# First mixer's output product: halves of the contraction by source, and the memory's transposes between the second halves

## The reference

```
x = x + hybrid_mixer(rms_norm(x, norm_mix_g), ...)      # [o_attention | h_mlstm] @ w_out
x = x + cross_attention(rms_norm(x, norm_x_g), rms_norm(mem, norm_mem_g), w_xq, w_xk, w_xv, w_xo)
```

## Time and profile before

| | us |
|---|---|
| median of 3 timed runs (1586.34 to 1586.98) | 1586.88 |
| the profiled execution's own time | 1581.93 |
| its span, first to last instruction | 1580.1 |
| TensorE busy in the span (matmuls) | 1350.8 |
| DVE / ACT / POOL busy | 536.6 / 413.6 / 423.5 |
| mean granted clock of TensorE, of full | 0.930 |

### The profile page before, as it was taken

One profiled execution on the slowest core, in us unless ns is written; L12 is line 12 of the kernel. 1 busy time (PEld: TensorE's weight loads), 2 busy tenths in 40 slices (PEclk: granted clock), 3 DMA queues, 4 the chain that ended last, 5 costly groups with the idle time before them and its releaser, 6 DMA issues. The chain is left out here.

```text
span 1580.1 us, 16473 instructions
## 1 busy us (share of the span) xinstructions
PE 1350.8 (85%) x6188; PEld 892.8 (57%) x6188; DVE 536.6 (34%) x1076; ACT 413.6 (26%) x796; POOL 423.5 (27%) x391
## 2 busy tenths in 40 slices
PE   6999976989889759987878888870999999999798
PEld 5777755788647633332223232220788887787466
DVE  3659657121061331111111111117141314563552
ACT  5323544144320200000000000014322223444441
POOL 7553340257410111211111111117144550000220
PEclk9999988999989759999999999995999999999799
DMA  7311212134202738999999999983132332232000
GB/s 198 107 54 55 106 54 80 59 128 148 92 4 98 315 159 337 422 420 424 420 423 421 424 421 423 422 344 120 54 107 80 107 100 81 87 105 82 1 21 34
DMA packets 72223, 297.73 MB, mean 188 GB/s; under 512 B 10152, under 2 KB 10200, under 8 KB 51424
## 3 DMA queue, kind: packets, MB, share of 16 engines
q1 hardware_dynamic: 64704, 282.27, 45.6%
q0 software_dynamic: 7456, 14.59, 2.9%
HBM read 292.63 MB, written 12.58 MB: 193 GB/s over the span
## 5 line engine op out<-in xcount | busy, mean ns | idle before, releaser
L703 POOL TENSOR_TENSOR ring_rounded<-ring,ring_rounded 128x512 fp32r<-128x512 f32 x208 | 284.9, 1404 | 326.1 <-ACT ring_rounded L1314 326.1
L826 PE MATMUL bank<-HT_rounded,ring_rounded 128*128 128x512 f32 x544 | 215.9, 397 | 4.3 <-DVE ring_rounded L1673 2.8
L1063 PE MATMUL bank<-ring,B 128*64 128x512 f32 x704 | 179.5, 663 | 44.2 <-DMA ring<-in_w 43.1
L828 PE MATMUL bank<-HT_rounded,ring_rounded 128*128 128x512 f32 x544 | 212.4, 390 | 0.0
L827 PE MATMUL bank<-ring_rounded 128*128 128x512 f32 x544 | 212.3, 390 | 0.0
L1063 PEld LDWEIGHTS bank<-ring,B 128*64 128x64 f32 x704 | 54.9, 150 | 152.4 <-issue 113.7
L828 PE MATMUL bank<-ring_rounded 128*128 128x512 f32 x352 | 137.9, 392 | 0.0
L1314 ACT ACTIVATE ring_rounded<-ring 128x2048 fp32r<-128x2048 f32 x56 | 106.4, 1915 | 111.4 <-DMA ring<-in_w_in_a 45.5
L2034 DVE TENSOR_TENSOR B<-bank,small 128x512 f32<-128x512 f32 x32 | 22.1, 692 | 331.7 <-PE bank L1053 331.7
L826 PEld LDWEIGHTS bank<-HT_rounded,ring_rounded 128*128 128x128 f32 x544 | 102.6, 189 | 32.2 <-issue 6.2
L827 PEld LDWEIGHTS bank<-ring_rounded 128*128 128x128 f32 x544 | 102.7, 189 | 21.7 <-issue 1.0
(11 more groups left out here) (362 smaller groups left out, 2034.4 us busy)
## 6 DMA issues: line engine op xcount, KB each, us to landing
ring<-in_w SPq DMA_DIRECT2D x88, 1024.0 KB, 30.3
A<-in_w SPq DMA_DIRECT2D x11, 2048.0 KB, 28.8
ring<-in_w SPq DMA_DIRECT2D x11, 2048.0 KB, 28.7
A<-in_w SPq DMA_DIRECT2D x20, 1024.0 KB, 28.8
HT<-in_w SPq DMA_DIRECT2D x20, 1024.0 KB, 32.2
XN<-in_w SPq DMA_DIRECT2D x10, 2048.0 KB, 28.9
ring<-in_w_in_a SPq DMA_DIRECT2D x16, 1024.0 KB, 5.0
ring<-in_w_in SPq DMA_DIRECT2D x14, 1024.0 KB, 7.3
```

What stands on the lines that cost most here:

```text
L703: last = pool.tensor_tensor(r32(lo), lo, r32_read(quarter(g, True)[:, k, :]), ALU.subtract)
L826: pe.matmul(o, r32(a_hi), r32(b_hi), start=first, stop=False)
L828: return pe.matmul(o, r32(a_lo), r32(b_hi), start=False, stop=last)
L1063: last = pe.matmul(bank[2 + b][64 * j:64 * j + 64, :], xgT[b][:, k, hf, :], w, start=(n == 0), stop=(n == 7), skip_group_check=True)
```

## The change

The output product's contraction is now taken by source. TensorE transposes the attention's four tiles, runs the first half of the contraction of `wo0` (channel tiles 0 to 3) for row tiles 0 to 2, transposes the cell's four tiles, runs row tile 3, then the first half of `wo1` for all four, the second half of `wo0`, the memory's transposes, and the second half of `wo1`. All eight banks are open at once in between. On DVE the attention's low parts come ahead of the cell's normalisation, and the additions of `wo1` behind the memory's low parts. On ACT the attention's high copies come ahead of the root and the memory's sums, and the memory's high copies ahead of the sums of the new x. In the plan, `opened` and `closed` become two lists, with four "skip" entries for banks that stay open.

```diff
     plan += [(("y_t", m), "dve") for m in range(8)]
-    plan += [(("wo", n, t), "dve") for n in range(2) for t in range(NT)]
+    plan += [(("wo", 0, t), "dve") for t in range(NT)]
     plan += [(("mem_t", k), "dve") for k in range(KD // 2)]
+    plan += [(("wo", 1, t), "dve") for t in range(NT)]
...
+    closed = [what for what, _ in plan]
+    opened = list(closed)
+    early = [("wo", 0, t) for t in range(NT)]
+    for what in early:
+        opened.remove(what)
+    at = opened.index(("y_t", 4))
+    opened[at:at] = early
+    late = [("wo", 1, t) for t in range(NT)]
+    for what in late:
+        opened.remove(what)
+    at = opened.index(("mem_t", 0))
+    opened[at:at] = [("skip", t) for t in range(NT)] + late
+    return opened, closed, dict(plan)
...
         last = opened[n - 8] if n >= 8 else None
+        if last and last[0] == "skip":
+            last = opened[n - 16]
...
-            for m in range(8):
+            def turn_y(m):
...
+            def out_half(outs, n, t, h):
+
+                part = weights(chunk_no[f"wo{n}"])
+                for k in range(4 * h, 4 * h + 4):
+                    last = passes(outs[t], lambda k: (yT[:, k, P * t:P * t + P], lowT[:, k, P * t:P * t + P]), part, k,
+                                  k == 0, k == KD - 1)
+                return last
+
+            for m in range(4):
+                turn_y(m)
+            outs = [[fill(U, "wo", 0, t)[:, :] for t in range(NT)]]
+            pe.wait_ge(sem("y_low_ready"), 4)
+            wait_split(pe, chunk_no["wo0"], 0)
+            for t in range(NT):
+                if t == NT - 1:
+                    for m in range(4, 8):
+                        turn_y(m)
+                last = out_half(outs[0], 0, t, 0)
+            last.then_inc(first_half_read, 1)
+            done[0] += NT
+            outs.append([fill(U, "wo", 1, t)[:, :] for t in range(NT)])
+            wait_split(pe, chunk_no["wo1"], 0)
+            for t in range(NT):
+                last = out_half(outs[1], 1, t, 0)
+            last.then_inc(first_half_read, 1)
             pe.wait_ge(sem("y_low_ready"), 8)
-            for n in range(2):
-                to_rows(f"wo{n}", U, [("wo", n, t) for t in range(NT)], yT, lowT)
-
+            wait_split(pe, chunk_no["wo0"], 1)
+            for t in range(NT):
+                out_half(outs[0], 0, t, 1).then_inc(bank_filled, 1)
...
+            wait_split(pe, chunk_no["wo1"], 1)
+            for t in range(NT):
+                out_half(outs[1], 1, t, 1).then_inc(bank_filled, 1)
             wait_emptied(pe, U["mem_t", KD // 2 - 1])
...
+            for m in range(4):
+                o = filled(U["y_t", m])
+                act.activation(r32(yT[:, m, :]), o[:, :], ACT.Copy, scale=g_sub_s).then_inc(sem("high_ready"), 1)
             roots(6, 48, 64)
...
             roots(7, NT, NT + MT)
             high_parts("xk0")
-            for t in range(NT):
-                wait_emptied(act, U["wo", 1, t])
-                sums(x_rows, t, 8 + t)
             act.wait_ge(sem("more_loaded"), 16 * 8)
...
+            for t in range(NT):
+                wait_emptied(act, U["wo", 1, t])
+                sums(x_rows, t, 8 + t)
             roots(8, 8, 8 + NT)
```

More of the change, by code:

```diff
@@ L167, in first_plan @@
     plan += [(("table",), "dve")]
-    return plan
+    closed = [what for what, _ in plan]
[11 more added lines that the diff above has]
+    return opened, closed, dict(plan)
 def second_plan():
@@ L237, in number @@
 def number(opened, closed, by, base, act0, dve0):
-    assert sorted(map(str, opened)) == sorted(map(str, closed))
+    assert sorted(str(what) for what in opened if what[0] != "skip") == sorted(map(str, closed))
     count, emptied = {"act": act0, "dve": dve0}, {}
@@ L246, in number @@
     for n, what in enumerate(opened):
+        if what[0] == "skip":
+            continue
         last = opened[n - 8] if n >= 8 else None
+        if last and last[0] == "skip":
+            last = opened[n - 16]
         after = (by[last], emptied[last]) if last else None
@@ L262, in build @@
 def build(nc, a, out):
[L264 to L267, removed]
+    opened1, closed1, by1 = first_plan()
+    n1 = len(closed1)
+    U, act1, dve1 = number(opened1, closed1, by1, 0, 0, 0)
     V, _, _ = number(*second_plan(), n1, act1, dve1)
@@ L1417, in _ @@
                 sums(mem_rows, t, NT + t)
[L1418 to L1425, removed]
+            for m in range(4, 8):
+                wait_emptied(act, U["y_t", m])
+                act.activation(r32(yT[:, m, :]), lowT[:, m, :], ACT.Copy).then_inc(sem("high_ready"), 1)
             roots(7, NT, NT + MT)
             high_parts("xk0")
-            for t in range(NT):
-                wait_emptied(act, U["wo", 1, t])
-                sums(x_rows, t, 8 + t)
             act.wait_ge(sem("more_loaded"), 16 * 8)
@@ L1833, in _ @@
                     head_rows(h - 1)
+            for m in range(4):
+                o = filled(U["y_t", m])
+                wait_high()
+                own(dve.scalar_tensor_tensor(r32(lowT[:, m, :]), o[:, :], g_sub_s, r32_read(yT[:, m, :]), ALU.mult,
+                                             ALU.subtract))
+                dve.nop().then_inc(done, 1)
+                dve.nop().then_inc(sem("y_low_ready"), 1)
             own(dve.tensor_scalar(ss[:, 48:64], mv[:, 1:32:2], float(P), None, ALU.mult))
@@ L1843, in _ @@
                 last.then_inc(sem("y_rows_ready"), 1)
-            for m in range(8):
+            for m in range(4, 8):
                 o = filled(U["y_t", m])
[L1846 to L1855, removed]
+                dve.wait_ge(sem("sig_ready"), m - 3)
+                dve.scalar_tensor_tensor(lowT[:, m, :], o[:, :], g_ml[:, m - 4:m - 3], moT[:, m - 4, :],
+                                         ALU.mult, ALU.mult).then_inc(done, 1)
             for m in range(4, 8):
@@ L1865, in _, with add_row @@
                    .then_inc(sem("memn_ready"), 1)
[L1867 to L1872, removed]
+            def add_row(name, n, t):
+                o = filled(U[name, n, t])
+                v = x_rows[:, t, 512 * n:512 * n + 512]
+                dve.tensor_tensor(v, o[:, :], v, ALU.add).then_inc(done, 1)
             dve.wait_ge(sem("x_again"), 16 * NT)
-            add_rows(U, "wo")
+            for t in range(NT):
+                add_row("wo", 0, t)
             dve.wait_ge(sem("more_loaded"), 16 * 8)
@@ L1884, in _ @@
                 last.then_inc(done, 1)
+            for t in range(NT):
+                add_row("wo", 1, t)
             rstds(NT, [(8, 8 + NT, D)])
@@ L1918, in _ @@
                                .then_inc(done, 1)
-            add_rows(U, "xw")
+            for n in range(2):
+                for t in range(NT):
+                    add_row("xw", n, t)
             rstds(NT, [(12, 12 + NT, D)])
```

## The result

| | before, us | changed, us |
|---|---|---|
| median of 5 timed runs | 1586.88 (1580.92 to 1587.98) | 1568.4 (1563.06 to 1571.4) |
| the profiled execution's own time | 1581.93 | 1563.06 |
| its span | 1580.1 | 1561.2 |
| mean granted clock | 0.930 | 0.940 |

The ratio is 0.99, 95% interval [0.9863, 0.9936]. The change gains; forecast were 13.1 us and 1573.8, with a range of 1571.3 to 1578.2.

A forecast was written before the change was run, and what follows sets the result against it. TensorE was taken as the bound except for two waits, ahead of the output product and the keys. Keys starting 11.4 us earlier plus 1.7 of kept clock gave 13.1 off 1586.88: 1573.8 us, range 1571.3 to 1578.2.

The forecast's parts named there:

- low clock behind that wait: At the output product's first matmuls after TensorE's idle wait: the lower clock costs 2.4 us, as before; ends 0 and 4.8.
- wait ahead of the keys: Before the keys' product: TensorE waits 1.4 us instead of 4.26, for DVE's fourth addition, and starts at 319.4.
- clock kept in the keys: In the keys' 192 matmuls: the short wait keeps the clock at 1.00, winning 1.7 us.
- the stages behind: After the keys: later work is tied to TensorE's own events and should move rigidly, with nothing further won or lost.
- my two ends: At the output product's start: the attention's four low parts take 4.66 us, or 4.3, winning 10.2 or 10.5 us.
- The transfer chain: Keys' weights: load from 305.5, 5.15 landing, 1.92 ACT copy, 4.17 memory copies and low parts, ending at 316.7.
- The cover for the second keys' weights: POOL's split of these weights: first half ready at 329.5, wanted at 330.9; slack 1.4 us, the next thing late.
- (a): Keys: the clock falls after the 1.4 us wait all the same; gain 11.4, 1575.5 us; chance 0.12.
- (b): Paired 1 MB loads share the engines, the first lands 2.5 us late; gain 8.9, 1578.0 us; chance 0.07.
- (c): Product's start: ACT's copies come only behind the root, DVE's first low part stays at 268.85; gain 8.1, 1578.8; chance 0.03.
- (d): Slower: the keys' load takes 30.3 us as in the expert stage; TensorE starts 13.8 us later, 1600.7; chance 0.03.
- I take 13.1 off both: Whole kernel: 13.1 us subtracted from profiled execution and timed median alike, giving 1568.8 and 1573.8 us.

The follow-up runs named there:

- the second trace: The changed kernel executed again without edits: ratio 0.9902 [0.9869, 0.9935] to the kernel before, median 1564.78 us of 6 runs, span 1569.0.
- the other three traces with before's order: Kernel before executed again, and with extra constant matmuls in two later waits (15 and 8; 8 and 5): ratios 0.9994, 1.0036, 0.9998.
- the first pair: First profiled executions of the kernel before and of the changed kernel: spans 1580.1 and 1561.2 us.
- the fillers: Extra constant matmuls in TensorE's waits; 4, 8 and 5 ahead of output product, cross attention and third norm in the changed kernel: 0.9867, median 1561.32 us.
- the parts apart: Against the kernel before: only the product by source, memory behind it as before, 0.9953; only the memory between the second halves, 0.9985.
- part 2 alone: Against the kernel before, memory's transposes between the second halves, all eight y tiles still transposed and split ahead of the product: 0.9985, median 1577.09 us.

## Why the prediction was right and wrong

**The mechanism and its size held.** The table gives the forecast's terms against what the runs showed, shifted by the 0.68 us of upstream where it is an instant.

| step | forecast | measured |
|---|---|---|
| start of the product | 268.5, 10.2 us won (10.5 as the bound) | 268.20, 10.5 us won |
| low clock behind that wait | 2.4 us (0 to 4.8) | 1.9 to 2.3 |
| both sets of transposes in the stream | 1.8 + 1.8 | product ends at about 317.9 (forecast 318.0) |
| wait ahead of the keys | 1.4, DVE's addition to X | 1.23 (1.60 in the second trace) |
| keys' start | 319.4 | 319.08 |
| clock kept in the keys | 1.7 | 1.5 (24.62 to 23.10); 1.3 against the other three traces with before's order |
| the stage | 13.1 | 13.2 in the first pair, 12.5 in the mean |
| the stages behind | 0, they "move rigidly" | 5.0 won in the first pair, 8.3 lost in the second |

That the first pair gives 13.2 is in part luck: before's first trace is the longest of the four with its order of the stage, by 1.0 us of clock. The start came near the lower of my two ends, 4.4 us after DVE's first low part, but by other terms: the four low parts take 3.99 us (the fourth starts 3.24 us after the first, with no long gap), and the handover to TensorE takes 0.41 where I had 0.05. The transfer chain landed where forecast, because its terms came from rows. The product ends at 318.40 − 1.23 = 317.17, with the shift 317.85. The cover for the second keys' weights held as well; POOL in order of time, the 8 pieces of these weights and the 8 of the next chunk in one group of 16, and the keys' 192 matmuls run through without a wait:

```profile
322.99 20.84 POOL L719 TENSOR_TENSOR ring_rounded<-ring,ring_rounded 128x512 fp32r<-128x512 f32 x16 [6.18 <-ACT ring_rounded L1360]
```

**The rivals fell.** (a), the clock falling after the short wait: 1.00 in all seven traces with such a wait, after 1.09 to 1.60 us. In the second trace of the changed kernel, in order of time and by a window:

```profile
317.83 0.35 PE L842 MATMUL bank<-A_rounded,ring_rounded 128*128 128x256 f32 x1 [1.60 <-DVE X L1914]
...
317.20:341.00 23.80, 23.17 (x193) 1.00 0.54 178
```

(b), the pair sharing the engines, fell with 5.2 us for the first of it. (c) fell with DVE's low part at 263.12. (d) fell with ACT on the weights at 309.76, 5.2 us after the issue at 304.52.

**The step that failed** is the first sentence of the numbers: "I take 13.1 off both", with the range built from the unknowns of the stage alone. It treats the median of three runs within 0.6 us of one another as the level of the kernel. It was not: all 81 runs of the kernel before in this case have a mean of 1580.0 and a median of 1578.3; 51 of them lie between 1574 and 1580, 23 in a tail from 1583 to 1590, and the three shown lay in that tail. The profiled execution already pointed at this, 4.95 us shorter than the median, and I noted the gap and carried it over unexplained. The changed kernel's five runs, 1563.06 to 1571.4, lie on both sides of its own mean. A range of ±3.5 us could not be relied on to hold a median of five from a kernel whose single executions differ by up to 15.5. Of the 18.5 us between the two medians 12.9 are the difference of the means; the first median stood 6.9 above its kernel's mean, the second 1.3 above its own.

The sign, and the size relative to before, are another matter. (1586.88 − 13.1) / 1586.88 is 0.9917: inside [0.9863, 0.9936] and inside [0.9869, 0.9935] of the second measurement. All 11 runs of the changed kernel have a mean of 1567.1, which is 12.9 below the 1580.0 of the 81. These are means over several chips and times, and the eleven scatter by 3.8 us, which leaves their mean uncertain by about 1.1 (an estimate from that scatter), so the agreement to 0.2 us is partly luck; the traces of the stage, 12.5 to 13.2, carry the claim.

**"Later stages move rigidly"** is the second step that failed: it was right of the schedule and wrong of the time, and it put at nothing a term that measured −5.0 us in the profiled pair and +8.3 in the second. Where the clock is the same, stages agree to 0.1 us (79.23 to 79.24 from the x1 transposes to the attention's in the traces without fillers). Where it isn't, the same thirty-two narrow matmuls cost 9.7 or 12.3 us.

**Still open:** what decides, in one execution, where the clock falls in the later stages, and why four of the first five runs of the kernel before lay at 1586 to 1588, where the three chips of the experiments have 11 of 39, 4 of 24 and 4 of 13 from 1583 up (chance, the chip or the time; no run tells them apart). Neither the fillers nor the parts apart fix it.

## What to carry to other kernels

When a product waits for all parts of its contraction, let it start on those that come from the source that is ready first, and move other sources' transposes into the matmul stream; look then for the next late thing, here the memory's chain behind a transfer, and give it the same treatment, because a third to a half of the profit at the end came from a wait short enough to keep the clock (1.3 of 3.8 us with part 2 alone, 1.5 of 2.7 in the first pair with both). Read a predicted or measured gain in its own stage, between marks that both traces have, and compare a second trace of the unchanged kernel before you credit a change with anything outside it. A few timed runs close together are not a level: if the profiled execution differs from them by more than half the width of your range (4.95 against 3.5 here), widen the range by that difference.

## What the runs showed of the hardware

- The spread between executions of one program on one core was up to 15.5 us in 1580 and goes with the mean granted clock: 1583 to 1590 us at 0.923 to 0.928, 1574 to 1580 us at 0.928 to 0.937.
- Thirty-two f32 matmuls of 36 columns (64 records) took 12.31 us in a stretch with a granted clock of 0.59 and 9.77 in one with 0.69, at the same place of the same kernel.
- A wait of 1.1 to 1.6 us ahead of the keys kept the clock at 1.00 in seven traces (23.1 us for the 192 matmuls behind it); one of 4.3 us brought it to 0.50 to 0.55, for a length that itself differed (24.4 to 25.6 us for the same 192 matmuls).
- Behind the waits of 7 and 8.5 to 9 us ahead of the product the clock was at the lower level for seven to twelve matmuls; with four fillers in the 7 us wait it was 1.00 from the first one on, and the stretch to the keys took 48.60 us instead of 50.54 to 50.88.
- A 512-column matmul of type f32 costs 0.86 us, in two records of 0.43, where one on rounded operands passes every 0.226 us: a filler of the plain type is nearly four times as long.
- Two loads of 1 MB issued together on one queue landed after 5.2 and about 8.4 us.
